# Input projection in plain fp32 matmuls, and the norms' sums of squares accumulated by TensorE

## What is computed

```python
def rms_norm(x, g):
    xf = x.astype(jnp.float32)
    y = xf * lax.rsqrt(jnp.mean(xf * xf, axis=-1, keepdims=True) + EPS)
    return (y * g.astype(jnp.float32)).astype(x.dtype)

def s5_mixer(h, w_in, log_dt, ...):           # first stage
    u = h @ w_in                              # the input projection, 1024 x 1024
    ...                                       # tables from dt and lambda, chunked scan, output
    val, gate = jnp.split(gelu(y) @ w_glu, 2, axis=-1)
    return val * jax.nn.sigmoid(gate)
...
for i in range(DEPTH):
    x = x + s5_mixer(rms_norm(x, ssm_norm), ...)      # i == 0
    x = x + diff_attention(rms_norm(x, attn_norm), k, v, ...)   # i == 1, k and v from rms_norm(x, kv_norm)
    x = x + conv_ffn(rms_norm(x, ffn_norm[i]), ...)
    x = x + sigmoid(rms_norm(x, ple_norm[i]) @ ple_w_gate[i]) * (p[i] @ ple_w_proj[i])
```

## Time and profile before

| | us |
|---|---|
| median of 3 runs | 1442.04 |
| the profiled execution, its own time | 1440.85 |
| its span, first to last instruction | 1439.1 |
| TensorE busy | 1324.1 (92%) |
| GpSimd busy | 1028.7 (71%) |
| VectorE busy | 768.7 (53%) |
| ScalarE busy | 688.3 (48%) |
| mean granted TensorE clock | 0.956 |

### The profile page before, as it was taken

How to read it: one execution, slowest core, us unless ns; L and a number is a source line. 1 busy time by engine, 2 the same in 40 slices (tenths; PEclk the granted TensorE clock), 3 DMA queues, 4 the chain that set the end, 5 groups by cost and what they waited for, 6 DMA issues and landing times.

```text
span 1439.1 us, 27942 instructions
## 1 busy us (share of the span) xinstructions
PE 1324.1 (92%) x10930; PEld 1275.0 (89%) x10930; DVE 768.7 (53%) x1254; ACT 688.3 (48%) x941; POOL 1028.7 (71%) x797
## 2 busy tenths in 40 slices
PE   4788999999979879999999768999999999899999
PEld 4777999999879658999999765999999998899999
DVE  7997775555673687755557586511114455611112
ACT  7613554344654675444446445544434544643342
POOL 1033988888768806888886663888887765788885
PEclk9889999999989879999999786999999999999999
DMA  6301555555437503555553430455554433355540
GB/s 247 160 18 35 203 181 180 189 187 175 147 135 203 194 14 103 185 189 175 177 189 135 154 134 32 138 185 177 186 192 176 148 124 118 118 179 189 187 146 29
DMA packets 33877, 217.05 MB, mean 151 GB/s; under 512 B 3683, under 2 KB 7428, under 8 KB 8196
## 3 DMA queue, kind: packets, MB, share of 16 engines
q1 hardware_dynamic: 29808, 209.05, 41.1%
q10 hardware_dynamic: 3988, 6.85, 1.8%
HBM read 213.26 MB, written 2.62 MB: 150 GB/s over the span
## 4 chain that ended last, share of the span: by engine, by line
PE 50%; POOL 19%; DVE 15%; issue 12%; ACT 3%; DMA 0%; DVEq 0%; POOLq 0%; ACTq 0%
POOL w_lo L335 18%; PE up L1329 12%; PE up L1331 12%; PE up L1330 12%; PE acc L1329 4%; PE acc L1331 4%; PE acc L1330 4%; DVE sq L779 2%; DVE x L1055 1%; DVE s_work L920 1%; ACT w_hi L397 1%; DVE mix L1215 1%; DVE mix L783 1%; DVE opnd L763 1%; DVE mix L1112 1%
## 5 line engine op out<-in xcount | busy, mean ns | idle before, releaser
L335 POOL TENSOR_TENSOR w_lo<-ring,w_hi 128x512 fp32r<-128x512 f32 x764 | 991.5, 1331 | 300.2 <-ACT w_hi L397 298.8
L1329 PE MATMUL up<-opnd,w_hi 128*128 128x256 f32 x2272 | 652.8, 287 | 23.2 <-DVE opnd L763 7.3
L1330 PE MATMUL up<-opnd,w_lo 128*128 128x256 f32 x2272 | 646.4, 285 | 0.0
L1331 PE MATMUL up<-opnd,w_hi 128*128 128x256 f32 x2272 | 646.2, 284 | 0.0
L397 ACT ACTIVATE w_hi<-ring 128x2048 fp32r<-128x2048 f32 x197 | 375.6, 1909 | 268.3 <-PE up L1331 208.7
L1329 PEld LDWEIGHTS up<-opnd,w_hi 128*128 128x128 f32 x2272 | 439.7, 194 | 30.9 <-issue 14.0
L1330 PEld LDWEIGHTS up<-opnd,w_lo 128*128 128x128 f32 x2272 | 439.7, 194 | 0.5
L1331 PEld LDWEIGHTS up<-opnd,w_hi 128*128 128x128 f32 x2272 | 439.6, 193 | 0.0
L1329 PE MATMUL acc<-opnd,w_hi 128*128 128x256 f32 x736 | 209.1, 284 | 5.3 <-DVE x L1028 2.7
L1330 PE MATMUL acc<-opnd,w_lo 128*128 128x256 f32 x736 | 208.3, 283 | 0.0
L1331 PE MATMUL acc<-opnd,w_hi 128*128 128x256 f32 x736 | 208.2, 283 | 0.0
(11 more groups left out here) (237 smaller groups left out, 1367.2 us busy)
## 6 DMA issues: line engine op xcount, KB each, us to landing
ring<-in_stream SPq DMA_DIRECT2D x197, 1024.0 KB, 4.9
bias_rows<-mix ACTq DMA_DIRECT2D x1, 1536.0 KB
x<-in_x SPq DMA_DIRECT2D x1, 1024.0 KB, 5.6
mix<-in_s_b ACTq DMA_DIRECT2D x1, 1024.0 KB, 9.5
mix<-in_s_c ACTq DMA_DIRECT2D x1, 1024.0 KB, 14.0
mix<-bias_rows ACTq DMA_DIRECT2D x1, 1024.0 KB, 5.7
out_x<-x SPq DMA_DIRECT2D x8, 128.0 KB, 1.7
mix<-in_p ACTq DMA_DIRECT2D x2, 256.0 KB, 2.6
```

The source lines that it names most:

```text
L335: ins = nc.gpsimd.tensor_tensor(w_lo[:, b, cols], ring[:, r, cols], w_hi[:, b, cols].bitcast(f32), ALU.subtract)
L1329: MM(o, l_hi, r_hi, start=start, stop=False, skip_group_check=True)
L1330: MM(o, l_lo, r_hi, start=False, stop=False, skip_group_check=True)
L1331: return MM(o, l_hi, r_lo, start=False, stop=stop, skip_group_check=True)
```

## The change

Two parts.

The input projection (`w_in`, slots 0 to 3) no longer splits anything: `whole_slot` multiplies the ring's fp32 weights by `ssm_x`, the scaled activations in fp32, with 16 plain fp32 matmuls a slot. The splits of x and of these four weight slots are gone from ScalarE and VectorE; `w_ready` for them is told by `evacuate`. The order at the start changes: VectorE makes `turns(0)` and `turns(1)` first, ScalarE makes `s5_tables(0)` ahead of `s_bn` and puts `s_bt` behind the norm, and TensorE puts slot 3 behind the second transposes. The sum of squares of this norm stays with VectorE.

For the nine other norms `add_square` is gone. TensorE instead multiplies every `sq[k]` by ones in the fresh slot, behind the six matmuls of the k tile, and accumulates the eight in PSUM; with tokens each k tile has two one-column matmuls more.

```diff
-            for m in range(KT):
-                c.up(A(hi("ssm")[:, m], x[:, m], ACT.Copy, scale=gain("ssm", m)), "hi_ready")
-            high_parts_to(0)
+            for m in range(KT):
+                c.up(A(ssm_x[:, m], x[:, m], ACT.Copy, scale=gain("ssm", m)), "ssm_ready")
...
-                if squares:
-                    add_square(m)
...
                 c.up_and_wait(TTo(dst, src, r, ALU.mult), "up_free")
+                c.tell("w_ready")
...
-            for m in range(KT):
-                low_tile("ssm", m, squares=False)
-            w_low(0)
+            dve.wait_ge(dma["s5_t"], 16)
+            turns(0)
+            turns(1)
             c.wait("mag", 2)
...
-            w_low(1)
-            w_low(2)
-            dve.wait_ge(dma["s5_t"], 16)
-            turns(0)
-            turns(1)
...
+            def square_sum(k, tokens):
+
+                c.wait("sq_ready")
+                ins = MM(aux[1][:, 0:T], ones, sq[:, k], start=(k == 0), stop=(k == KT - 1), skip_group_check=True)
+                if tokens:
+                    for t in range(TT):
+                        ins = MM(aux[0][:, t:t + 1], sq[:, k, t * P:(t + 1) * P], ones[:, 0:1],
+                                 start=(k == 0 and t == 0), stop=(k == KT - 1), skip_group_check=True)
+                if k == KT - 1:
+                    c.up(ins, "ssq")
...
+                    if sums and k < KT - 1:
+                        square_sum(k, False)
                 c.up(ins, "mm_done")
+                if sums:
+                    square_sum(KT - 1, False)
...
-            up_slot("ssm", S, fresh=True)
+            def whole_slot(s, fresh=False):
+
+                pe.wait_ge(ring_full[s], 16)
+                o = bank()
+                for k in range(KT):
+                    if fresh:
+                        c.wait("ssm_ready")
+                    for m in range(2):
+                        ins = MM(o[:, m], ring[:, s, (2 * k + m) * P:(2 * k + m + 1) * P], ssm_x[:, k],
+                                 start=(k == 0 and m == 0), stop=(k == KT - 1), skip_group_check=True)
+                c.up(ins, "mm_done")
+
+            whole_slot(S, fresh=True)
...
-            rms(adds=3)
-            up_slot("ssm", S + 1)
-            up_slot("ssm", S + 2)
-            up_slot("ssm", S + 3)
+            c.up(MM(aux[1][:, 0:T], ones, sq[:, 0], start=True, stop=True), "ssq")
+            whole_slot(S + 1)
+            whole_slot(S + 2)
...
                 c.up(ins, "s5_ab_ps")
+            whole_slot(S + 3)
             c.wait("s5_cm", 4)
```

More of the change, by code:

```diff
@@ L40 @@
     _u += {"ffn": 2 * STEPS, "ple": 4}.get(_name[:3], _n)
[L43 removed]
+UNITS = ["s5", "ffn0", "ple0", "kv", "q", "diff", "ffn1", "ple1", "even", "mixed", "ffn2",
          "odd", "stick", "ffn3"]
 UNIT = {n: i for i, n in enumerate(UNITS)}
[L46 removed]
+SET = dict(s5=1, ffn0=0, ple0=0, kv=1, q=0, diff=1, ffn1=0, ple1=0, even=1, mixed=1,
            ffn2=0, odd=0, stick=1, ffn3=0)
@@ L167, in program @@
             pass
-        opnd = [sb(f"opnd{i}", [P, 2, KT, T], f32r) for i in range(2)]
+        opnd = [sb("opnd0", [P, 2, KT, T], f32r)]
+        with nc.sbuf_tensor("ssm_x", [P, KT, T], f32) as ssm_x:
+            pass
+        opnd.append(sb("opnd1", [P, 2, KT, T], f32r))
         acc = ctx.enter_context(nc.psum_tensor("acc", [P, 4, 512], f32))
@@ L352, in _ @@
             first = START["glu"] + 2
-            c.wait("w_hi_ready", first)
+            c.wait("w_hi_ready", first - START["glu"])
             c.wait("w_ready", first)
@@ L388, in _ @@
             A = nc.scalar.activation
-            ahead = [0]
+            ahead = [START["glu"]]
             def high_part(s, i=None):
@@ L486, in _ @@
             s5_tables(0)
+            c.wait("s5_bt_ps", 2)
+            b_ps = [acc[:, 2 * r:2 * r + 2].rearrange("p a (b c) -> p (a b) c", c=32) for r in range(2)]
+            for r in range(2):
+                for h in range(2):
+                    part, cols = own(b_ps[r], h)
+                    c.up(A(own(s_bn, h)[0][:, r], part[:, :, cols], ACT.Copy, scale=1.0 - 2.0 * r), "s5_bn")
+            c.wait("lam_sum")
+            c.up(A(lam_e, aux[1][:, 0:2], ACT.Exp), "lam_exp")
+            c.wait("eps")
+            rms()
+            for r in range(2):
+                c.up(A(s_bt[:, r], b_ps[r], ACT.Copy, scale=1.0 - 2.0 * r), "s5_bt")
+            act.wait_ge(dma["s5_c"], 16)
+            for h in range(2):
+                part, cols = own(s_craw, h)
+                c.up(A(own(s_cn, h)[0], part[:, :, :, cols], ACT.Copy), "s5_cn")
             s5_tables(1)
@@ L758, in step, with low_tile @@
                 c.up_and_wait(ins, "dve_step")
-            def low_tile(name, m, squares=True):
+            def low_tile(name, m):
                 c.wait("hi_ready")
@@ L885, in _ @@
             evacuate(0)
-            w_low(3)
             c.wait("s5_cn", 2)
@@ L1061, in ple @@
                     for m in range(KT):
-                        low_tile(name, m, squares=False)
+                        low_tile(name, m)
             def residual(name, S, u0):
@@ L1396, in down_slot @@
                 return ins
-            def rms(tokens=False, adds=KT - 1):
-                c.wait("sq_sum", adds)
-                ins = MM(aux[1][:, 0:T], ones, sq[:, 0], start=True, stop=True)
-                if tokens:
-                    for t in range(TT):
-                        ins = MM(aux[0][:, t:t + 1], sq[:, 0, t * P:(t + 1) * P], ones[:, 0:1], start=True, stop=True)
-                c.up(ins, "ssq")
             pe.wait_ge(dma["par"], 16)
@@ L1508, in ffn @@
                 assert used[0] == BANK[f"ffn{l}"]
-                up_slot(name, S, fresh=True)
-                rms()
+                up_slot(name, S, fresh=True, sums=True)
                 up_slot(name, S + 1)
@@ L1541, in ple @@
                 for g in range(4):
-                    up_slot(f"ple{l}", S + g + 1, fresh=(g == 0))
-                    if g == 0:
-                        rms()
+                    up_slot(f"ple{l}", S + g + 1, fresh=(g == 0), sums=(g == 0))
             def head_stats(n, sq_r, half_r, banks):
```

48 lines of the change are left out of this document (14 added, 34 removed).

## The result

The changed kernel takes **1420.74 us** (median of 4 runs, 1419.47 to 1422.62) against 1442.16 of the kernel before (4 runs, 1440.53 to 1443.99): a ratio of 0.985, 95% interval 0.9835 to 0.9869. Forecast were 1428.0 and a range of 1420 to 1436. The direction held, and of the mechanism the start and the `ple` stages; the size was 21.4 us by the medians where 14.0 had been forecast, which is outside the forecast's own range of 1424 to 1432 and 0.7 us inside the wide one. What follows is told against these 19.4. In experiment 7 one of the six executions of the kernel with "table and tokens, all fp32" took 2142.48 us at a granted clock of 0.556; it moves that kernel's median by 0.1 us.

What follows compares the result with a forecast made beforehand. TensorE, busy 92% of the span, was taken as the bound, with waits for VectorE. Start -6, feed-forward norms +2.5, `odd` +2.5, `ple` stages -12.0, cold beginnings -1: -14.0, so 1428.0 us; own range 1424 to 1432, wide 1420 to 1436.

Steps and rivals of the forecast that it cites:

- The start: From kernel begin to first scan: dropping splits brings the scan 6.3 us earlier; 6 taken, ends 3 and 8.
- the start gives nothing: Before `glu`: ScalarE or VectorE waits elsewhere, or plain matmuls run at half clock; -8 in all, 1434 us; chance 0.09.
- The four feed-forward norms: Fresh slots of `ffn0` to `ffn3`: TensorE alone sets their end; +1.8, -0.1, +0.3 and +0.5, sum +2.5 us.
- cold beginnings: Slots behind `ffn1` and `ffn3`: low-clock starts (0.91, 0.92) vanish if TensorE runs through; some -1 us.
- 8 x (0.72 + 0.48) = 9.6 us: Fresh slot before a feed-forward layer: eight k tiles, each 0.72 us of matmuls plus a 0.48 us sum.
- `odd`: Fresh slot with tokens, directly behind a down slot: 12.2 us of TensorE work against 9.68, so +2.5 us.
- VectorE's relief is worth nothing here: In the `odd` slot: VectorE needs some 3 us less than its 8.08, but TensorE needs 12.2.
- The `ple` stages: Two stages: each -2.2 in down slots, -3.0 in the stretch (39.0 against 42.0), -0.8 behind; together -12.0 us.
- The lock keeps VectorE's pace: `ple` stages: shared-port lock with GpSimd's splits keeps VectorE's groups at 8.1 us; 8.4 us gained in all, 1433.6; chance 0.17.
- TensorE pays more per sum: Fresh slots: a sum costs 0.9 instead of 0.48 us, +30, 1457 us; decides at 0.67 us; chance 0.07.
- No net change: Whole kernel: gains come at half and sums cost 0.6 us; chance 0.04.
- More than forecast: Whole kernel: start gives 8 us, VectorE is never behind, the clock stays up throughout; 1421 us; chance 0.08.

Runs made afterwards that it cites:

- experiment 7: Combinations on the changed kernel: earlier table with token norm from rstd and one-pass sums, 1402.38 us; with token norm only, 1413.19; with one-pass sums only, 1397.91.
- table and tokens, all fp32: Changed kernel with the third `s5_tables` group ahead of `k0` and the norm by token turned from `rstd`, sums still four-pass fp32: 1413.19 us.
- experiment 1: Changed kernel with the nine norms' sums by VectorE again: 1436.77 us; changed kernel with the old start but TensorE's sums: 1428.36 us.
- Experiment 2: Changed kernel with sums by VectorE's adds again, in the four `ffn` norms alone: 1423.17 us; in the `odd` norm alone: 1419.77 us.
- Experiment 6: Changed kernel, but VectorE also adds two squares per tile into unused memory in `ple0`, `kv`, `ple1` and `even`: 1437.36 us.

## Why the prediction held in direction and missed in size

- **The start** (forecast 6, range of terms 3 to 8): 5.8 at the scan, 6.4 at `ffn0`, 5.6 by experiment 1. Slot 0 at 9.4, `k0` at 49.75 instead of 49.2. The plain matmuls cost 0.44 us (slot 3, 42.75 to 49.75) where 0.43 was taken. The 1.5 us for table load and exponential was a guess without a row; the norm's sum starts 4.0 us after the end of the transposes, as the forecast had it (24.97 instead of 24.3). The rival that the start gives nothing is out.
- **The four feed-forward norms** (forecast +2.5, and -1 for cold beginnings). This is the term that was mis-sized. The step took "8 x (0.72 + 0.48) = 9.6 us"; the sum costs 0.43 us where it lies between k tiles, and the first matmul behind a sum already starts 0.24 us after it (371.60 to 371.84), so the slot, from start to start, is 0.96 + 7 x 1.15 = 9.0 us. That is 0.6 less, four times, or 2.5 us: the forecast's whole loss. Its +0.3 for `ffn2` had no row; before, that stretch took 9.32 us (914.27 to 923.59). `ffn0` lost 1.15, `ffn1` gained 0.70, `ffn2` 0.36, `ffn3` 0.25, in sum 0.2 gained; behind `ffn1` and `ffn3` it was 0.7 and 0.9 (before, the slots there began at a clock of 0.82 and 0.79 in their first 4.5 us, after at 1.00). Experiment 2 has the group at 2.4 us in favour of TensorE.
- **`odd`** (forecast +2.5). Locally +3.0, as 0.87 was paid for sum and columns instead of 0.80. The step that failed is that this loss stays: the forecast looked at the slot alone, and behind it 2.1 us came back through the length of one VectorE instruction. "VectorE's relief is worth nothing here" is true of the slot and not of what follows. Net +0.7 to +1.0 (the two traces, experiment 2).
- **The `ple` stages** (forecast -12.0): -12.9, of which 2.1 in each down slot (forecast 2.2), 2.9 in each stretch (3.0), and 1.2 and 1.7 in the slots behind (0.8). 39.08 us against 39.0 is partly luck, since the sum without tokens was put too dear and the one with tokens too cheap: the two fresh slots took 8.97 (370.88 to 379.85) and 12.65 us (397.31 to 409.96) where 9.6 and 12.2 stood in the sum. Experiment 6 shows the cause.
- **Not forecast:** 1.3 us were lost between the slots behind `kv` and `ffn1`. All of it comes in one place, the attention's last transposes and values and two k tiles of its output slot, which took 7.16 us at a clock of 1.00 before and 8.53 at 0.80 after. Before, then after:

```profile
529.74:536.90 7.16, 5.07 (x29) 4.08 (x30) 5.16 (x13) 6.72 (x23) 0.00 (x0) 1.00 0.00 1
```

```profile
518.29:526.82 8.53, 6.44 (x29) 5.46 (x30) 5.47 (x14) 7.17 (x23) 0.00 (x0) 0.80 0.00 0
```

  The matmuls there start 0.21 us apart instead of 0.12. Why the clock fell in one and not in the other, with nearly the same waits ahead, was not tried.
- **The rivals.** *The lock keeps VectorE's pace*: partly seen, in that one group of three has three long instructions and takes 7.0 us, but TensorE has no wait there. From group to group it was 5.3, 7.0 and 5.0 us, where about 6 had been forecast. As the forecast argued, it settles between, and experiment 6 shows how near the edge lies: one more instruction for each tile is enough. *TensorE pays more per sum*: out, 0.43 against its 0.67. *No net change* is out. *More than forecast* (1421, chance 0.08) is where the time fell, though by another way than "the start gives 8": the start gave 6, and the rest came from the fresh slots, from what `odd` got back, and from the clock.

In sum: start -6.4, `ffn` norms -1.8 with the clock behind them, `ple` -12.9, attentions +1.0, `odd` with what came back +0.7, together -19.4. Of the 5.4 us beyond the forecast 3.3 are the `ffn` norms, 1.8 `odd`, 0.9 `ple` and 0.4 the start, less the 1.0 of the attentions. The further 2.0 us by which the medians differ are in no trace.

## What to carry to other kernels

Price an operation that goes between the matmuls of a stream by the distance that it adds there, not by the gap behind a lone one: the forecast took the gap, and that made four slots 2.5 us too long, the whole of a term. Once the engine that took over the work is the one that sets the pace, its passes are what is left: the same sums in one pass were worth as much again (22 us) as the whole change. And before work is taken off an engine, look at what the other engines do in the time that goes: 2.9 us more in one slot were given back by 2.1, and 2.9 us less in it cost 3.9 in another kernel, by how long a VectorE instruction stood behind GpSimd's splits.

## What the runs showed of the hardware

The same VectorE instruction, 128 x 768 with both inputs in SBUF, took 1.91 or 1.92 us in ten kernels and 3.98 to 4.33 in four. It always began in the middle of one of GpSimd's splits, and ended 0.81 or 0.82 us after the end of one. What differs is how many it stood behind. In the long cases it was three, the running one and the last two of the block (ends 1115.83 and 1116.65, 1100.55 and 1101.37). In the changed kernel it was one, though GpSimd's block went on for as long: 3.08 us from VectorE's start (1118.29 to 1121.37) against 3.16 in the kernel with `odd` by VectorE (1112.67 to 1115.83). There VectorE came in ahead of the last split. The Trainium skill, "SBUF — State Buffer", Who interferes with whom, gives the pair of ports that the two engines share as an exclusive lock, held for a whole instruction, with the order of issue deciding who blocks. The trace agrees that either blocks the other (GpSimd's last split took 2.02 us instead of 1.3 where VectorE came first), and shows more than that: VectorE can stand behind three splits in a row, while the 1.51 us of an add in the earlier trace rows is about 0.4 and one split. What decides whether VectorE gets in between two splits stays open; the gap in GpSimd's run (experiment 2) goes with it in all fourteen kernels.
